# Mixing the two maps of differential attention with adding DMAs, and a bias band of 308 columns

## The reference, cut to what matters

```python
table = rel_bias[:, :DIFF_HEADS].T
def block(args):                       # one block of 128 queries, all 4 heads
    qb, bi = args
    qpos = bi * BLOCK + jnp.arange(BLOCK)
    bias = table[:, t5_bucket(kpos[None, :] - qpos[:, None])]
    sc = jnp.einsum('bqhmd,bkhmd->bmhqk', qb, k) * scale + bias[None, None]
    p = jax.nn.softmax(sc, axis=-1)    # two maps, m = 0 and 1
    a = p[:, 0] - lam * p[:, 1]
    return jnp.einsum('bhqk,bkhd->bqhd', a, v)
```

## Time and profile before

| | |
|---|---|
| median of 3 runs | 3987.99 us (3985.63 to 3988.3) |
| the profiled execution | 3982.62 us, span 3980.7 us |
| mean granted TensorE clock | 0.982 of full |
| TensorE busy | 95% |
| GpSimd, VectorE, ScalarE busy | 58%, 55%, 44% |
| transfers | 392.49 MB, 99 GB/s in the mean |
| differential attention, exponentials | layer 0 from 1185.9 us; layer 1 to 3626.4 us |

### The profile page before, as it was taken

One profiled execution on the slowest core, in us unless ns is written; L12 is line 12 of the kernel. 1 busy time (PEld: TensorE's weight loads), 2 busy tenths in 40 slices (PEclk: granted clock), 3 DMA queues, 4 the chain that ended last, 5 costly groups with the idle time before them and its releaser, 6 DMA issues. The chain is left out here.

```text
span 3980.7 us, 52431 instructions
## 1 busy us (share of the span) xinstructions
PE 3792.6 (95%) x19002; PEld 2645.2 (66%) x19002; DVE 2181.2 (55%) x3979; ACT 1747.5 (44%) x3140; POOL 2294.8 (58%) x1381
## 2 busy tenths in 40 slices
PE   8999999999989999889989999999999899998899
PEld 8789775555546666557887897755555466665577
DVE  3003125655559999775540031255555599997755
ACT  3102103433339999770031021023333499997610
POOL 1221325877768999644612213257777699996355
PEclk9999999999999999999999999999999999999999
DMA  5334445232411222245454344432224202223353
GB/s 179 124 124 130 137 140 131 65 81 60 100 43 26 58 58 59 61 110 192 150 167 124 126 127 138 140 80 56 56 61 103 54 8 58 58 59 81 105 178 136
DMA packets 180871, 392.49 MB, mean 99 GB/s; under 512 B 18014, under 2 KB 100168, under 8 KB 168968
## 3 DMA queue, kind: packets, MB, share of 16 engines
q1 hardware_dynamic: 179752, 387.75, 35.0%
q10 hardware_dynamic: 864, 1.41, 0.2%
HBM read 255.93 MB, written 135.67 MB: 98 GB/s over the span
## 5 line engine op out<-in xcount | busy, mean ns | idle before, releaser
L1327 POOL TENSOR_TENSOR mla_sum_pool<-mla_sum_pool,mla_probs 128x1024 f32<-128x1024 f32 (+1 forms) x336 | 777.8, 2315 | 207.3 <-ACT mla_probs L1288 182.2
L1345 DVE TENSOR_REDUCE carry_row_max<-psum 128x1 f32<-128x512 f32 x688 | 474.6, 690 | 414.2 <-PE psum L1160 409.2
L1288 ACT ACTIVATE mla_probs<-psum 128x1024 f32<-128x1024 f32 x384 | 373.3, 1021 | 694.0 <-PE psum L1197 689.3
L1723 POOL TENSOR_TENSOR diff_probs<-diff_probs 128x1024 f32<-128x1024 f32 x252 | 597.1, 2369 | 100.5 <-ACT diff_probs L1667 90.0
L1655 ACT ACTIVATE diff_probs<-psum,diff_shift 128x1024 f32<-128x1024 f32 x384 | 425.7, 1115 | 11.3 <-DVE diff_shift L1750 10.0
L655 PE MATMUL psum<-in_x_hi,in_w_hi 128*128 128x512 f32 x1024 | 409.1, 399 | 2.7 <-ACT in_mla_val L763 2.7
L655 PE MATMUL psum<-in_x_hi,in_w_lo 128*128 128x512 f32 x1024 | 405.9, 396 | 0.0
L655 PE MATMUL psum<-carry_firsts,in_w_hi 128*128 128x512 f32 x1024 | 405.9, 396 | 0.0
L1210 PE MATMUL psum<-mla_probs,mla_v_op 128*64 128x512 f32 x1536 | 373.2, 607 | 0.0
L1594 PE MATMUL psum<-ident,diff_probs 128*128 128x128 f32 x2048 | 319.5, 279 | 15.1 <-DVE diff_turned L1785 8.5
L1740 DVE TENSOR_REDUCE diff_part_shift<-psum 128x1 f32<-128x1024 f32 x256 | 311.3, 1217 | 26.9 <-PE psum L1568 19.0
(11 more groups left out here) (248 smaller groups left out, 7400.9 us busy)
## 6 DMA issues: line engine op xcount, KB each, us to landing
in_w_raw<-in_w_in SPq DMA_DIRECT2D x64, 512.0 KB, 3.9
split_d<-in_out SPq DMA_DIRECT2D x32, 512.0 KB, 2.7
split_d<-handed SPq DMA_DIRECT2D x32, 512.0 KB, 2.7
carry_firsts<-split_d SPq DMA_DIRECT2D x48, 256.0 KB, 8.0
carry_weights<-split_d SPq DMA_DIRECT2D x48, 256.0 KB, 7.7
carry_weights<-split_d SPq DMA_DIRECT2D x16, 768.0 KB, 18.3
carry_rows<-in_x SPq DMA_DIRECT2D x16, 512.0 KB, 3.7
raw_d<-in_out SPq DMA_DIRECT2D x16, 512.0 KB, 2.7
```

Source lines behind the costliest of these rows:

```text
L1288: nc.scalar.activation(probs[:, s % RING, :].rearrange("p (a n) -> p a n", n=CH), psum[:, S0 + 2 * (s % 2):S0 + 2 * (s % 2) + 2, :], ACT.E ...
L1327: nc.gpsimd.tensor_tensor(acc, start, probs[:, s % RING, mine], ALU.add).then_inc(pool_added, 1)
L1345: nc.vector.tensor_reduce(row_max[:, u % 2, qb, n:n + 1], psum[:, sweep_bank(g), :], AX.X, ALU.max).then_inc(maxed, 1)
L1723: nc.gpsimd.tensor_tensor(probs[:, n % DEEP, at], probs[:, n % DEEP, at], second, ALU.add).then_inc(mixed, 1)
```

## The change

Three things change in the differential attention. First, the sums on GpSimd (L1723) go, but for the second half of the last two units; in their place GpSimd issues DMAs from `probs1` to `probs`, both in SBUF, which add what they carry to what stands in their destination (`accum_op=ALU.add`), 128 rows of 1024 floats each, two for a unit. Their completions count on `first_added` and `added`, two semaphores each, by the parity of the unit. `turns` and `exp` wait for those in place of `mixed`, and GpSimd waits for the one of unit n-2 before it issues that of n. Second, ScalarE no longer scales: GpSimd scales all 1024 columns of the second half. Third, the band narrows from 384 to 90 + 128 + 90 = 308 columns. The constant part now covers also the neighbouring blocks (`left`, `right` from one block away), and for that the tables of these two blocks have the far constant subtracted, by eight VectorE instructions in the latent attention of layer 0, with `far` now loaded to all 128 partitions.

```diff
...
 REL_W = 4 * P - 1
+REACH = 90
 NORM0, NORM1 = MLA_HEADS * DV // P, (MLA_HEADS + DIFF_HEADS) * DV // P
...
             rows = sb("rows", [32, 2])
-            far = sb("far", [32, 2, BIAS_HEADS])
+            far = sb("far", [P, 2, BIAS_HEADS])
             far_acc = sb("far_acc", [32, DIFF_HEADS, NB])
...
                 sem(n) for n in ("t_loaded", "rel_psum", "rel_ready", "rel_stored", "skewed", "toeplitz"))
-            masked, tiles_hi_ready, tiles_lo_ready, chain, by_block, side_ready, t_stored = (
-                sem(n) for n in ("masked", "tiles_hi_ready", "tiles_lo_ready", "chain", "by_block", "side_ready",
+            centred, masked, tiles_hi_ready, tiles_lo_ready, chain, by_block, side_ready, t_stored = (
+                sem(n) for n in ("centred", "masked", "tiles_hi_ready", "tiles_lo_ready", "chain", "by_block", "side_ready",
                                  "t_stored"))
...
                     for n, bucket in enumerate((REL_BUCKETS // 2 - 1, REL_BUCKETS - 1)):
-                        sp.dma_start(far[:, n, :], rel_bias[bucket:bucket + 1, :].partition_broadcast(32)
+                        sp.dma_start(far[:, n, :], rel_bias[bucket:bucket + 1, :].partition_broadcast(P)
                                      ).then_inc(t_loaded, 16)
...
                         for h in range(DIFF_HEADS):
-                            nc.vector.tensor_scalar(far_acc[:, h, :], sides[:, 0, :], far[:, 0, h:h + 1], None, ALU.mult
+                            nc.vector.tensor_scalar(far_acc[:, h, :], sides[:, 0, :], far[0:32, 0, h:h + 1], None, ALU.mult
                                                     ).then_inc(chain, 1)
                             dve.wait_ge(chain, 2 * h + 1)
-                            nc.vector.scalar_tensor_tensor(far_acc[:, h, :], sides[:, 1, :], far[:, 1, h:h + 1],
+                            nc.vector.scalar_tensor_tensor(far_acc[:, h, :], sides[:, 1, :], far[0:32, 1, h:h + 1],
                                                            far_acc[:, h, :], ALU.mult, ALU.add).then_inc(chain, 1)
...
                         dve.wait_ge(toeplitz, 16 * BIAS_HEADS)
+                        for h in range(DIFF_HEADS):
+                            for n, side_of in enumerate((slice(0, P), slice(2 * P, 3 * P))):
+                                nc.vector.tensor_scalar(tiles[:, h, side_of], tiles[:, h, side_of], far[:, n, h:h + 1],
+                                                        None, ALU.subtract).then_inc(centred, 1)
+                        dve.wait_ge(centred, 2 * DIFF_HEADS)
                         nc.vector.tensor_copy(tiles_hi[:, :, :], tiles[:, 0:DIFF_HEADS, :]).then_inc(tiles_hi_ready, 1)
...
             sem(n) for n in ("scored", "maxed", "shifted", "exped", "summed", "inverted", "ratio_ready"))
-        parted, act_scaled, late_ready = (sem(n) for n in ("parted", "act_scaled", "late_ready"))
+        parted, late_ready, added, first_added = sem("parted"), sem("late_ready"), two("added"), two("first_added")
         times_ratio, mixed, turn_done, pv_done, odd_out, o_ready = (
...
             def band_pieces(qb):
-                lo_, hi_ = max(qb - 1, 0) * P, min(qb + 2, NB) * P
+                lo_, hi_ = max(qb * P - REACH, 0), min((qb + 1) * P + REACH, SEQ)
                 cuts = [lo_] + [c for c in range(CH, SEQ, CH) if lo_ < c < hi_] + [hi_]
...
                         return
-                    if n < LATE:
-                        pe.wait_ge(mixed, 2 * n + c // 2 + 1)
+                    if n < LATE and c < 2:
+                        pe.wait_ge(first_added[n % 2], 16 * (n // 2 + 1))
+                    elif n < LATE:
+                        pe.wait_ge(added[n % 2], 16 * (n // 2 + 1))
                     elif c < 2:
...
                     else:
-                        pe.wait_ge(mixed, 2 * LATE + n - LATE + 1)
+                        pe.wait_ge(mixed, n - LATE + 1)
                     if n < LATE or (n, c) == (LATE, 0):
...
                         if n >= DEEP1:
-                            act.wait_ge(mixed, 2 * (n - DEEP1 + 1))
+                            old = n - DEEP1
+                            act.wait_ge((added if half else first_added)[old % 2], 16 * (old // 2 + 1))
                     dst = probs[:, n % DEEP, :] if m == 0 else probs1[:, n % DEEP1, :]
...
                                          bias=shift[:, n % 2, 1:2], scale=-1.0).then_inc(parted, 1)
-
-                def scale(n):
-                    act.wait_ge(ratio_ready, n + 1)
-                    first = probs1[:, n % DEEP1, HALF:HALF + CH]
-                    nc.scalar.activation(first, first, ACT.Copy, scale=ratio[:, n % 2:n % 2 + 1]).then_inc(act_scaled, 1)
                 def copy(n, c):
...
                         parts(n)
-                    if 1 <= n <= UNITS:
-                        scale(n - 1)
             @block.gpsimd
...
                     done = 2 * n if n < LATE else LATE + n
-                    for k, half in enumerate((0, 1) if n < LATE else (1,)):
-                        at = slice(half * HALF, (half + 1) * HALF)
-                        second = probs1[:, n % DEEP1, at]
-                        factor = part[:, n % DEEP1:n % DEEP1 + 1] if half == 0 else 1.0
-                        mine = second if half == 0 else probs1[:, n % DEEP1, HALF + CH:SEQ]
-                        nc.gpsimd.tensor_scalar(mine, mine, ratio[:, n % 2:n % 2 + 1], factor, ALU.mult, ALU.mult
+                    first, second = probs1[:, n % DEEP1, 0:HALF], probs1[:, n % DEEP1, HALF:SEQ]
+                    factor = ratio[:, n % 2:n % 2 + 1]
+                    if n < LATE:
+                        nc.gpsimd.tensor_scalar(first, first, factor, part[:, n % DEEP1:n % DEEP1 + 1], ALU.mult, ALU.mult
                                                 ).then_inc(times_ratio, 1)
-                        pool.wait_ge(times_ratio, done + k + 1)
-                        if half == 1:
-                            pool.wait_ge(act_scaled, n + 1)
-                        nc.gpsimd.tensor_tensor(probs[:, n % DEEP, at], probs[:, n % DEEP, at], second, ALU.add
+                        pool.wait_ge(times_ratio, done + 1)
+                        if n >= 2:
+                            pool.wait_ge(first_added[n % 2], 16 * (n // 2))
+                        pool.dma_start(probs[:, n % DEEP, 0:HALF], first, accum_op=ALU.add
+                                       ).then_inc(first_added[n % 2], 16)
+                    nc.gpsimd.tensor_scalar(second, second, factor, 1.0, ALU.mult, ALU.mult).then_inc(times_ratio, 1)
+                    pool.wait_ge(times_ratio, done + (2 if n < LATE else 1))
+                    if n < LATE:
+                        if n >= 2:
+                            pool.wait_ge(added[n % 2], 16 * (n // 2))
+                        pool.dma_start(probs[:, n % DEEP, HALF:SEQ], second, accum_op=ALU.add).then_inc(added[n % 2], 16)
+                    else:
+                        nc.gpsimd.tensor_tensor(probs[:, n % DEEP, HALF:SEQ], probs[:, n % DEEP, HALF:SEQ], second, ALU.add
                                                 ).then_inc(mixed, 1)
                 pool.wait_ge(o_ready, (H - 1) * (NB // 2))
-                pool.wait_ge(mixed, LATE + UNITS)
+                pool.wait_ge(mixed, UNITS - LATE)
                 nc.gpsimd.memset(carry["keys_lo"][SWA_DIM:P].bitcast(F32), 0.0).then_inc(carry_sems["zeroed"], 1)
...
                         dve.wait_ge(times_ratio, 2 * (n - 1))
-                        dve.wait_ge(act_scaled, n - 1)
                     nc.vector.tensor_scalar(ratio[:, n % 2:n % 2 + 1], inv1[:, n % 2:n % 2 + 1],
...
     kb, qb = np.arange(NB)[:, None], np.arange(NB)[None, :]
-    left, right = kb <= qb - 2, kb >= qb + 2
+    left, right = kb <= qb - 1, kb >= qb + 1
     lo_rows = (np.arange(2 * NB) >= NB).astype(f32)
...
```

## The result

| | before | after |
|---|---|---|
| median | 3987.05 us (3985.63 to 3988.3, 4 runs) | 4092.28 us (4090.72 to 4097.32, 4 runs) |
| profiled execution, span | 3982.62, 3980.7 us | 4091.4, 4089.6 us |
| differential attention, layer 0 (first to last shift) | 454.2 us | 509.3 us |
| the same, layer 1 | 454.3 us | 511.7 us |

The ratio is 1.0265, 95% interval 1.0253 to 1.0277. The forecast was 3962 us, range 3935 to 4065: wrong in sign, and outside the range. The last two rows of the table are measured from the first to the last of the 64 instructions on VectorE that write `diff_shift` from `diff_row_max`, one a unit (63 unit lengths); I call the distance of two of them a unit. The two stages are 55.1 + 57.4 = 112.5 us longer, the span 108.9: all of the loss, and a little more, is in the stage that the change touches.

The account below looks back on a forecast made before the run. Bound taken: the loop of ScalarE, TensorE and VectorE round three PSUM score slots. Savings of 31 us in units and 2 at the ends, costs of 1 for tables and 6 for head loads: 26 us net, 3962 us, range 3935 to 4065.

Parts of the forecast that it names:

- plus 6 for the head loads (about 1 us for each of six): Differential attention: six head loads beside the adding DMAs cost about 1 us each, 6 us added to the time.
- rival 1: Head loads make additions late: six loads at 11 to 12 us each, net +38, about 4026 us; chance 0.26.
- the prediction's own sign: TensorE's turns waiting for GpSimd's DMA queue only inside the head-load windows would show the head loads make additions late.
- so they wait for their 32 destination partitions, and additions can pass: Head loads move 215 GB/s at full share, fastest slice 387; so additions can pass, hence 1 us a load.
- The gain of 31 us: Differential attention: 0.11 (band) plus 0.14 (score waits) is 0.25 us a unit, over 126 units 31 us.
- ScalarE's relief, taken as 0.14 us a unit: Without ScalarE's scale, mostly TensorE's wait for free score banks comes back: 7.9 us over 55 units, 0.14 a unit.
- The band, 0.11 us a unit: Narrowing the band matmuls from 384 to 308 columns saves a mean 0.11 us a unit, all on TensorE.
- the third rival: The loop does not loosen: only the band shows, half lost to loads, 3 to 8 us remain, 3982; chance 0.12.
- landing taken at 4 us: Each 512 KB adding DMA in SBUF takes 4 us to landing, 2.7 of them on the queues' engines.
- The slack of 2.1 us in quiet units: First half: TensorE turns it 8.3 us after the ratio; scale, issue and landing take 6.2, leaving 2.1 us.
- the second rival: Additions slower than a unit can hide: 4.9 us each, 328 us over 126 units, about 4316; chance 0.12.
- The terms of 1 us for the tables and 2 us at the ends: VectorE's table subtractions in layer 0's latent attention cost 1 us; the stage ends gain 1 us per layer, 2 in all.

Follow-up runs that it names:

- Experiment 6: Changed kernel with only the second half added by DMA, GpSimd adding the first half again and still doing all scaling: 4057.1 us, ratio 1.0178.
- 3: Changed kernel with operands of heads 1 to 3 loaded for 64 of 2048 columns, loads for the windowed attention whole: 4019.37 us, ratio 1.0067.
- 4: Changed kernel with each head load's transfers issued one by one over nine units (windowed attention's over eight), same bytes: 4020.73 us, ratio 1.0072.
- 14: Changed kernel with every load beside the additions cut to 2 KB rows and issued spread over nine units (keys eight): 4003.54 us, ratio 1.0039.
- experiment 5: Changed kernel with each operand transfer of 32 rows of 8 KB made 128 rows of 2 KB over all partitions: 4040.7 us, ratio 1.0132.
- experiment 2: Kernel before without ScalarE's scale of 512 columns and the waits for it, nothing in its place: 3979.4 us, ratio 0.9971.
- experiment 1: Kernel before with only the band of 308 columns and its tables, mixing unchanged: 3980.69 us, ratio 0.9976.
- 9: Kernel before with the 308-column band, ScalarE's copy of turned quarter 0 cut from 512 to 128 columns: 3969.5 us, ratio 0.9958.
- 10: Kernel before with the 308-column band, ScalarE's copy of quarter 2 cut to a fourth of its columns: ratio 0.9990.
- 13: Changed kernel with operands, constant rows and windowed attention's keys cut to 2 KB rows, four transfers in place of one: 4020.1 us, ratio 1.0074.
- 12: Changed kernel with only the operand transfers cut to 2 KB rows, four in place of one, same 32 partitions: 4050.54 us, ratio 1.0159.

## Why the prediction was wrong

**The term that failed: "plus 6 for the head loads (about 1 us for each of six)".** Measured: 16.3 to 17.5 us for each of six, and 7.5 and 8.6 for the loads at the stages' starts, 117 us in all. This was rival 1, that the head loads make the additions late, and by the prediction's own sign: TensorE waits for the additions only at the loads. Its price was too low as well. It had six loads at 11 to 12 us, from sharing the engines by halves. The halves are about right: in after, from 1328 to 1340 us, the loads' queue has 52.4% of the engines and the additions' 48.3%. But eight loads cost, and more each. What counts is how long one addition takes: in layer 0 up to 18.1 us, against the 7.3 to 8.2 after which TensorE asks. And the rival had no term for the lower clock behind the waits, which makes TensorE's own work 14.6 and 18.6 us longer. Experiment 6 shows that a load delays even a lone addition, 3 that without the loads' bytes the stalls go, 4 that they mostly go when the load is spread over time; 4 and 14 together, that the length of its rows counts too, but less.

The forecast put its main chance against this on one observation: the loads move 215 GB/s at a full share where 387 is possible, "so they wait for their 32 destination partitions, and additions can pass". The first half may be so (experiment 5 reaches 425 GB/s with 128 partitions); the second does not follow. Once an addition's rows run, the transfers show turns: in experiment 6 95 rows of the load stand between 128 of the addition, and these take 5.4 us in place of 2.4. The Trainium skill, DMA: Bandwidth & Descriptors, "Queues, rings and completion order", states such turns: each engine goes round between its queues packet by packet and drains a packet before it switches. By that rule an addition of many rows pays a turn of the load again and again. The trace agrees for this part of the delay. It is not the whole: the first row starts up to 6.9 us after the issue in place of 1.5, while the load alone fills the engines, and why it can't begin sooner no run here shows.

**The gain of 31 us that was not there.** *ScalarE's relief, taken as 0.14 us a unit:* zero (experiment 2, and after's own quiet units). The forecast read in its own rows that the exponential could start only 0.1 us sooner, because VectorE's shift came at 1414.96, and then credited TensorE's wait for score banks all the same. That wait belongs to the exponential behind copy 0, and the scale is not in that loop. *The band, 0.11 us a unit:* 0.04 (experiment 1). The matmuls did shorten as worked out; in the timeline of after

```profile
1394.51 0.45 PE L1574 MATMUL psum<-carry_weights,ident_r 128*128 128x308 f32 x2
1394.79 0.63 PE L1568 MATMUL psum<-carry_weights 128*128 128x512 f32 x2
```

is 0.28 us for a pair, as foretold. But most of what TensorE saves does not shorten the unit, whose length the loop through ScalarE sets. In this the third rival, that the loop does not loosen, was right: 5 us in the units. That both errors of the sum have one origin, the loop, is argued from 2, 9 and 10; no run makes the loop itself shorter with the work unchanged. Four engines at 90 to 97% do not say which instructions form the loop.

**What held.** The additions in quiet stretches: landing taken at 4 us, measured 5.0 (4.6 where they are half as many); engines' time taken at 2.7 us each, measured 0.79 of 7.2 us for two, 2.8 each. The prediction had also weighed the fixed part and the rate of the Trainium skill, DMA: Bandwidth & Descriptors, "Anatomy of one DMA", with the half rate of an adding DMA from the Trainium skill, Collectives: The Full Stack, "The bandwidth ceiling": an estimated 4.4 us to landing and 2.4 of the engines. Both measurements are above it. The issue on GpSimd, taken at 1 us, is 0.89, and its scale of 1024 columns 1.18 and 1.44:

```profile
L1725 POOL TENSOR_SCALAR diff_probs<-diff_probs,diff_ratio 128x1024 f32<-128x1024 f32 x48 | 69.2, 1441 | 0.0
...
L1730 POOL DMA_DIRECT2D diff_probs<-diff_probs x49 | 43.4, 886 | 14.5 <-POOL diff_probs L1725 14.5
```

The slack of 2.1 us in quiet units was enough, and the second rival, additions too slow in every unit, did not come. The terms of 1 us for the tables and 2 us at the ends were not tried alone; outside the two stages after is 112.5 - 108.9 = 3.6 us shorter, so neither shows a loss.

**What stays open.** Why 14 still exceeds the band alone by 16.7 and 10.0 us a layer. Engines filled to 97% leave an addition little room, and some transfers in that stage (the store of each head, the band, the values, the queries of the windowed attention) were not cut; neither was tried by itself. Open is also why the first row of an addition starts so late beside a load. And open is how much of 5 comes from the 128 partitions. The run to set beside it is 13, whose operands and constant rows are cut to 2 KB as in 5 (12 keeps 8 KB for the constant rows): the first three loads of layer 0 cost 14.9 us in 5 and 9.2 in 13, of layer 1 14.9 and 14.0. So no gain from more partitions shows; but 13 spreads its issues over some 52 us and 5 over some 22, and no run varies the partitions alone. How the stage would do with the additions but a full clock was not tried either: 14.6 and 18.6 us is TensorE's longer work, not a measured price.

**The version to keep** is the band alone, experiment 1: the only one of these with nothing left out that isn't slower than before. Its ratio of 0.9976 is small, and experiment 2 has 0.9971 with unchanged units; what speaks for it is that its units are shorter one by one, 2.6 and 2.3 us a layer.

## What to carry to other kernels

Work moved from an idle-looking engine to the DMA queues takes on a latency that is set by whatever else is queued there: price it at the busiest transfer of the stage, against the distance from its issue to its first reader, not against the mean share. If it must share with bulk loads, spread those over time; shorter rows come second, and more transfers are themselves a spread. Count TensorE's waits at more than their length: here its granted clock was at the lower level for a while behind them. And before crediting a shortened instruction, follow the loop through it: the same cut of ScalarE's work brought 5.5 and 8.2 us a layer in one place and next to nothing in another.

## What the runs showed of the hardware

- An adding DMA of 512 KB within SBUF, issued by GpSimd, holds GpSimd 0.89 us, lands after 4.6 to 5.0 us and takes 2.8 us of all 16 engines, where the plain store of that size lands after 2.7 us.
- Beside loads of 8 KB rows on SP's queue, 12 issues in 12.7 us, it lands after 11.8 us (median; single ones in layer 0 up to 18.1). With the load spread over 43.6 us it lands after 6.7, with 2 KB rows over 45.8 us after 6.9 (1340 to 1400 us), and in equal stretches of 80 us after 6.7 with 8 KB and 6.0 with 2 KB rows, both spread.
- Alone beside such a load, an addition's first row starts 3.0 to 6.9 us after the issue (1.5 in quiet), and its rows alternate with the load's, 128 to 95, over 5.4 us (2.4 in quiet).
- An issue on SP holds its queue about 1 us each in this load: 12 take 12.7 us, 48 take 45.8, so that cutting a load in pieces also spreads it.
- Loads into 32 partitions run at some 215 GB/s with the engines' share at 1.00; with the same bytes into 128 partitions, additions and loads together reach 316 to 425 GB/s in single slices.
- TensorE's granted clock was 0.50 from 1339.8 to 1346.4 us, after it had begun to stand for an addition (4.4 us, until 1341.9), and 1.00 in the 93 us of the stage without such waits; over the stage of layer 0 it was at the lower level 47.8 us, before 6.8.
